# The delta rule's chunk inverse: products with 32 stationary columns in four tiles of 64x32, in place of 64 in two of 64x64

## What is computed

```python
def step(s, xs):
    qc, kc, vc, gc, bc = xs
    gcum = jnp.cumsum(gc, axis=-1)
    diff = gcum[..., :, None] - gcum[..., None, :]
    kb = kc * bc[..., None]
    a = -jnp.einsum('bhid,bhjd->bhij', kb, kc) * jnp.exp(jnp.where(strict, diff, -jnp.inf))
    rhs = jnp.concatenate([kb * jnp.exp(gcum)[..., None], vc * bc[..., None]], axis=-1)
    sol = lax.linalg.triangular_solve(eye - a, rhs, left_side=True, lower=True, unit_diagonal=True)
    w, u = sol[..., :dk], sol[..., dk:]
    v_new = u - w @ s
    attn = jnp.einsum('bhid,bhjd->bhij', qc, kc) * jnp.exp(jnp.where(incl, diff, -jnp.inf))
    o = (qc * jnp.exp(gcum)[..., None]) @ s + attn @ v_new
```

## Time and profile before

| what | value |
|---|---|
| time, median of 3 runs | 3820.77 us (3820.32 to 3820.97) |
| profiled execution, its span | 3819.8 us |
| profiled execution, time outside its span | about 1.0 us, by the median of the runs, 3820.77 us |
| TensorE matmul busy | 3704.5 us (97%), 19284 instructions |
| TensorE weight loads busy | 2362.5 us (62%) |
| VectorE busy | 1739.2 us (46%) |
| ScalarE, GpSimd busy | 969.9 us (25%), 612.5 us (16%) |
| DMA | 72 GB/s over the span |
| granted TensorE clock | 0.98 of 2.4 GHz on average |

### The profile page before, as it was taken

The page is one execution under the profiler, slowest core; times in us unless marked ns, Lnnn a source line. Parts: engine busy times, 40 slices in busy tenths (PEclk is TensorE's granted clock), DMA queues, the critical chain, the costliest instruction groups (busy, mean ns, idle before and its releaser), DMA issues.

```text
span 3819.8 us, 48291 instructions
## 1 busy us (share of the span) xinstructions
PE 3704.5 (97%) x19284; PEld 2362.5 (62%) x19284; DVE 1739.2 (46%) x3861; ACT 969.9 (25%) x1804; POOL 612.5 (16%) x549
## 2 busy tenths in 40 slices
PE   7999999989999999999999999999999999999999
PEld 3578885864476444444444468876664558876654
DVE  3877763365453233333334654522541374523531
ACT  5223322232100310000003512311551321312531
POOL 4001210140000222222223202211001101311001
PEclk8998999989999999999999999999999999999999
DMA  6301112155354111111111303310001412310021
GB/s 204 131 10 29 32 53 80 51 176 168 132 171 163 44 44 44 44 44 44 44 44 34 145 23 97 92 56 25 1 35 54 147 43 79 99 59 23 1 83 44
DMA packets 216173, 276.51 MB, mean 72 GB/s; under 512 B 27453, under 2 KB 174488, under 8 KB 215312
## 3 DMA queue, kind: packets, MB, share of 16 engines
q1 hardware_dynamic: 202336, 205.18, 17.3%
q0 software_dynamic: 13616, 68.24, 4.7%
HBM read 238.58 MB, written 34.81 MB: 72 GB/s over the span
## 4 chain that ended last, share of the span: by engine, by line
PE 88%; DVE 6%; ACT 2%; issue 2%; DMA 1%; POOL 0%; DVEq 0%; POOLq 0%; ACTq 0%
PE ps L3296 18%; PE ps L3167 9%; PE ps L1049 9%; PE ps L4258 7%; PE ps L1071 6%; PE ps L4551 4%; PE ps L4728 3%; PE ps L2925 3%; PE ps L1136 2%; PE ps L4208 2%; PE ps L4785 2%; PE ps L4768 2%; PE ps L3364 1%; PE ps L1826 1%; PE ps L1842 1%
## 5 line engine op out<-in xcount | busy, mean ns | idle before, releaser
L3296 PE MATMUL ps<-big 128*128 128x512 f32 x1624 | 697.1, 592 | 0.0
L3296 PEld LDWEIGHTS ps<-big 128*128 128x128 f32 x1624 | 308.6, 190 | 388.4 <-issue 385.5
L1049 PE MATMUL ps<-big 128*128 128x512 f32 (+1 forms) x1056 | 403.7, 543 | 0.0
L3167 PE MATMUL ps<-big 128*128 128x512 f32 (+1 forms) x896 | 359.3, 562 | 3.4 <-DVE big L4915 2.4
L1049 PEld LDWEIGHTS ps<-big 128*128 128x128 f32 x1056 | 200.1, 191 | 197.3 <-issue 190.9
L3167 PEld LDWEIGHTS ps<-big 128*128 128x128 f32 x896 | 169.6, 190 | 188.0 <-issue 182.4
L3489 DVE SCALAR_TENSOR_TENSOR big<-ps,big 128x512 f32<-128x512 f32 x212 | 159.0, 750 | 242.8 <-PE ps L3296 208.8
L4258 PE MATMUL ps<-big 128*128 128x256 f32 x1152 | 252.6, 379 | 0.0
L4258 PEld LDWEIGHTS ps<-big 128*128 128x128 f32 x1152 | 217.2, 190 | 29.3 <-issue 0.7
L1071 PE MATMUL ps<-big 128*128 128x256 f32 (+1 forms) x1344 | 228.2, 332 | 0.0
L1071 PEld LDWEIGHTS ps<-big 128*128 128x128 f32 x1344 | 207.7, 191 | 19.7 <-issue 1.0
(11 more groups left out here) (509 smaller groups left out, 5470.6 us busy)
## 6 DMA issues: line engine op xcount, KB each, us to landing
big<-in_w_mlp SPq DMA_DIRECT2D x32, 1024.0 KB, 5.3
big<-in_w_in SPq DMA_DIRECT2D x29, 1024.0 KB, 5.5
big<-in_w_mod SPq DMA_DIRECT2D x24, 1024.0 KB, 5.8
big<-in_w_ada SPq DMA_DIRECT2D x24, 1024.0 KB, 8.3
big<-us_scratch SPq DMA_DIRECT2D x72, 256.0 KB, 4.5
hs_scratch<-big POOLq DMA_DIRECT2D x3, 5120.0 KB, 17.4
big<-c_dft SPq DMA_DIRECT2D x12, 1024.0 KB, 5.6
xs_scratch<-big POOLq DMA_DIRECT2D x16, 640.0 KB, 4.2
```

The costliest lines, as they stand in the source:

```text
L1049: t = e.matmul(b[:, 0:n], wv[:, k, 128 * m:128 * m + 128], K.hT[:, k, t0:t0 + n], start=(k == 0), stop=(k == 7))
L3167: t = e.matmul(b[:, 0:n], wv[:, k, c:c + 128], cat[:, k, t0:t0 + n], start=(k == 0), stop=(k == 7))
L3296: t = e.matmul(z, w[:, k, c], y, start=(first and k == 0), stop=(k == nk - 1), skip_group_check=not first)
```

## The change

In `left` and `right` every product with 64 stationary columns is written as two with 32: the first takes stationary columns 0 to 31 of the head and writes the lower 32 of the 64 output partitions, the second columns 32 to 63 and the upper 32. The new helper `rows` gives those output partitions. The moving operand is the same for both and is streamed twice. The order is head, then column half x, then half p of the partitions, so neighbouring products go to different tiles of the array: four tiles of 64 rows by 32 columns for n below 6 (two of 64x64 before), two for n = 6 (one before). The increment of the semaphore stays on the last product. All other engines' code is the same.

```diff
--- before.py
+++ after.py
@@ -1810,6 +1810,9 @@
             t = e.matmul(b[J, 256 + 64 * h:320 + 64 * h], k4[:, h, J], k4[:, h, I], start=True, stop=True)
         t.then_inc(P.sem, P.up(("mm", u)))
 
+    def rows(self, p, x):
+        return slice(p.start + 32 * x, p.start + 32 * x + 32)
+
     def left(self, place, n):
         e, P, d, c, ch = self.e, self.P, self.d, self.chunk(place), self.ch
         J, I = self.J, self.I
@@ -1819,11 +1822,14 @@
         e.wait_ge(*self.at(*self.key("X", d, c, n - 1)))
         for h in range(4):
             sl = slice(64 * h, 64 * h + 64)
-            if n == 6:
-                t = e.matmul(b[I, sl], ch["LT"][J, 256 + 64 * h:320 + 64 * h], ch["X"][J, sl], start=True, stop=True)
-                continue
-            for p in self.halves:
-                t = e.matmul(b[p, sl], ch["LT"][p, sl], ch["X"][p, sl], start=True, stop=True)
+            for x in range(2):
+                cols = slice(64 * h + 32 * x, 64 * h + 32 * x + 32)
+                if n == 6:
+                    t = e.matmul(b[self.rows(I, x), sl], ch["LT"][J, 256 + cols.start:256 + cols.stop], ch["X"][J, sl],
+                                 start=True, stop=True)
+                    continue
+                for p in self.halves:
+                    t = e.matmul(b[self.rows(p, x), sl], ch["LT"][p, cols], ch["X"][p, sl], start=True, stop=True)
         t.then_inc(P.sem, P.up(("mm", u), self.key("left", d, c, n)))
 
     def right(self, place, n):
@@ -1835,11 +1841,14 @@
         e.wait_ge(*self.at(*self.key("M1", d, c, n)))
         for h in range(4):
             sl = slice(64 * h, 64 * h + 64)
-            if n == 6:
-                t = e.matmul(b[J, sl], M1[I, sl], XT[I, sl], start=True, stop=True)
-                continue
-            for p in self.halves:
-                t = e.matmul(part(b[p, 32 * h:32 * h + 32]), M1[p, sl], half(XT[p, sl], 1 - d), start=True, stop=True)
+            for x in range(2):
+                cols = slice(64 * h + 32 * x, 64 * h + 32 * x + 32)
+                if n == 6:
+                    t = e.matmul(b[self.rows(J, x), sl], M1[I, cols], XT[I, sl], start=True, stop=True)
+                    continue
+                for p in self.halves:
+                    t = e.matmul(part(b[self.rows(p, x), 32 * h:32 * h + 32]), M1[p, cols], half(XT[p, sl], 1 - d),
+                                 start=True, stop=True)
         t.then_inc(P.sem, P.up(("mm", u)))
 
     def queries(self, place):
```

## The result

The changed kernel takes 3834.73 us (median of 7 runs, 3831.04 to 3841.51), the kernel before, run beside it on the same chip, 3820.77 us (median of 7, 3809.17 to 3825.42). The ratio is 1.0039, 95% interval 1.0028 to 1.0050: slower by 14 us. The prediction said 3806 us and faster. The time lies inside its range, the sign does not. The profiled execution is the fastest of the seven, 3831.04 us, so the trace shows some 10 us of these 14.

What follows compares the result with a forecast made beforehand. TensorE bounds the stage, with VectorE only 13 us a period to spare. Chain gains of 18.5 and 1.8 us plus first loads make 22, times 0.69 is 15: 3819.8 - 15.2 = 3804.6, plus 1.0, 3806 us; range 3790 to 3838.

Steps and rivals of the forecast that it cites:

- Added: 3520 pairs, 7040 instructions: Extra TensorE instructions in the left and right batches, fetched on a queue of their own: no cost.
- The array's part: Left and right batches on TensorE: 7.9 and 14 ns a pair, right batches 21 us shorter in all, left 2 us.
- rival 2: Column tiles of one row group take turns in left and right batches: some 40 us slower, 3861 us; chance 0.04.
- the prediction's sum: Whole program: the profiled execution falls by 15.2 us, from 3819.8 to 3804.6 us.
- 22 x 0.69: Gain on the chain of waits, 22 us, times the 69% left after VectorE's cover in one round: 15 us.
- Rival 1: TensorE isn't fed pairs faster than 29.2 ns in the loop's rounds: 22 us more, 3841 us; chance in full 0.15.
- the feeding rival: Rival 1: TensorE isn't fed fast enough in the loop's rounds, 3841 us; chance in full 0.15.
- Rival 3: Granted clock: one more 1.2 GHz stretch costs 12 us, 3818 us; two, 3830 us (chance 0.05); or one goes, 3794 us.
- Rival 4: VectorE takes nearly all the gain in the loop: 3814 to 3821 us; within a shared no-change chance of 0.19.

Runs made afterwards that it cites:

- right_only: The changed kernel with `left` put back as before, so only right products with n below 6 are split (1600 added pairs): 3809.47 us, 0.9979 of before.
- right_shift: right_only with 128 more semaphore instructions on TensorE at the program's start, all on a value long reached: 3813.31 us, 0.9993 of before.
- pad: The kernel before with 3200 added pairs, products of 32 stationary and one moving column into unused bank columns beside the old 64x64 products: 4252.62 us, 1.1128 of before.

## Why the prediction was wrong

**The step that failed** is "Added: 3520 pairs, 7040 instructions. They are fetched on a queue of their own", "at no cost". It read the queue's share, 0.9%, as cover, and the term was put at nothing. The share says that the queue isn't full; it doesn't say how soon the next packet can come. The supply has two numbers, 256 instructions a packet and about 3.4 us between two starts, and the kernel before never came near the second (closest 4.41 us, median 6.8). The change brought the median to 4.1 us and the closest to 3.35, and at 31 of the scan's 68 packet borders (none of 40 before) TensorE stood still until the next packet had landed: 31.1 us where the prediction had 0.

**The array's part was right.** Rates of 8.6 and 14.0 ns a pair against 7.9 and 14; a right group of 96 pairs without a stall 1.06 us against 1.0 expected; the left one 1.43 us for 87 pairs, which at its rate is 1.56 for 96 against 1.55. The change of column tiles (rival 2) doesn't show.

**The sum at full clock** is an estimate from the two windows of the stage. TensorE ran at 1.2 GHz for 47.2 us of it before and 31.3 after; with half of that taken off, before is 299.9 - 23.6 = 276.3 us, after 310.8 - 15.6 = 295.2 us, and without the 31.1 us at borders 264.1: 12 us less than before, where the prediction's sum was 15.2. The measured 10.9 us of the stage are then -12 for the array with VectorE's part, +31 for the stalls, and -8 for the clock. This is good to a few us: a stall may have covered a wait for VectorE that would show without it, and with all 35 gaps counted the array's part would be 16. So how much VectorE takes back, for which the prediction had 22 x 0.69, isn't measured by any run. The clock lay in the other direction: in the profiled execution of before it was at 1.2 GHz for 27.3 us from 347 us on, in that of after for 3.4 and 6.8 us (a stretch of 24 to 27 us that begins near the scan's end is in both).

**Rival 1** had the right engine, the right sign and nearly the price, 3841 us, with a chance of 0.15. Its picture was not right. It had the supply as a rate, a pair in no less than 29 ns, and looked for a right group of over 2 us. In truth batches run at 8.6 ns a pair as long as their instructions are there, and the 26.6 ns hold over a packet. Its other sign, gaps inside batches without a wait, is what the trace shows. What was argued against it, single pairs 20 ns apart in the earlier trace rows, was true and told nothing: 8 matmuls are a small part of a packet. The rule of the Trainium skill that the prediction cites, that start to start never drops below about 25 ns, is contradicted by 87 left pairs in 1.43 us (14 ns) and 32 right ones in 0.46.

The Trainium skill, "Runtime: NRT & Kernel Launch", section "Instruction fetch mechanics", has the block of 16 KiB and 256 instructions, and a prefetch of the next block while the present one runs; the remainders and packets here agree. It also says that crossing a block's border is mostly hidden, since engines dispatch more slowly than the fetch fills. With TensorE at 4 to 7 ns an instruction, this trace has 31.1 us of stalls at such borders.

**Rival 3**, the clock, was priced right in kind (12 us a stretch; 27.3 us at half speed are 13.7) but mostly expected in the wrong direction: apart from the scan's end, the clock was low for 10.2 and 13.6 us in the two executions of after, for 27.3 and 34.1 in those of before. It hid part of the loss. **Rival 4** doesn't explain the loss: VectorE's busy time is the same 210 us, and the idle time of TensorE that VectorE ended rose by 1.5 us in front of `left` (L1997 and L2026, 14.0 us for 12.5) and by 1.3 us in front of `right`.

**Could the profile of before have told?** The distance of packets, yes. The stage fetched 40 packets in 300 us, 4.41 us apart at the closest. A round with 208 pairs after the change, 416 instructions or 1.6 packets, was to be run in 4.3 us: 2.6 us a packet, nearer than any two packets in the trace. That comparison, demand of the densest stretch against the closest packets seen, was missing. It would not have shown a limit, since the 4.41 us were set by what the kernel before asked for; but it would have shown that the change leaves what this trace covers, and so that the feeding rival deserved far more than 0.15.

**No better version.** Of the kernels that keep all of the reference's products, right_only has the lowest median, 0.9979 of before. But right_shift, the same products with the borders elsewhere, has 0.9993, and their intervals overlap. The gain to be had this way is 0.2% at most, and part of it depends on where packets happen to end.

## What to carry to other kernels

Splitting products into smaller tiles buys array time with instructions. Before doing so, work out how long the densest stretch takes for each 256 of TensorE's instructions, and hold that against the distance of the instruction packets in the trace; the queue's share of time tells nothing. Where 256 instructions would be used up in less than some 3.4 us, TensorE stalled in these kernels; where slow products stand between the fast batches, it mostly did not. An "issue" gap in the middle of a batch, at the same instruction in two executions, is the mark to look for.

## What the runs showed of the hardware

- TensorE's instructions arrive 256 to a packet, no two closer than 3.34 us in any execution, and 3.34 to 3.42 us at the closest in seven of the ten executions with added pairs; in the kernel after, a stall at a border ends 2.2 to 2.8 us after the packet's start and 1.2 to 1.6 us after its landing, and the next packet starts 1.15 us later at the earliest.
- Four tiles of 64 rows by 32 columns run a pair of fp32 load and matmul every 8.6 ns with 32 moving columns, and every 14 ns with 64.
- Neighbouring products in tiles of different shape (64x32 and 64x64) cost some 0.1 us more per change than those of one shape: 0.42 us for 4 + 4 pairs against 0.23 us for 8 (pad, at full clock).
- The granted clock's stretch at 1.2 GHz moves by 30 us between two executions of one kernel, and the kernel before took 3808 to 3810 us at a mean clock of 0.988 and 3823 to 3824 us at 0.983.
- With TensorE busy for 99.5% of a stretch of 738 us, the granted clock was 1.2 GHz for 710 us of it (pad).
